# Laying out the large weights on the host so that a load's share of each partition is one run

## The reference, cut to what matters

```
mod = silu(c) @ w_ada + b_ada                      # w_ada 1024 x 6144
h = rmsnorm(x) * (1 + scale1) + shift1
q_A, k_A, v_A, f_A, q_B, k_B, v_B = split(h @ w_in) # w_in 1024 x 3080
oA = forgetting attention (prompt causal; samples over 2048 paged past rows)
oB = dilated window attention (samples over a window buffer, which is returned shifted by one row)
x = x + gate1 * (concat(rmsnorm(oA), rmsnorm(oB)) @ w_o)   # w_o 1024 x 1024
h2 = rmsnorm(x) * (1 + scale2) + shift2
s = sigmoid(h2 @ w_router); 8 of 64 experts per row, limited by groups
routed = sum over the chosen experts e: gate * (silu(h2 @ w_gate[e]) * (h2 @ w_up[e])) @ w_down[e]
shared = (silu(h2 @ ws_gate) * (h2 @ ws_up)) @ ws_down
x = x + gate2 * (routed + shared)
```

## Time and profile before

| | |
|---|---|
| time, median of 3 runs | 1496.65 us (1496.37 to 1498.79) |
| the profiled execution's own time | 1504.03 us |
| its span | 1502.3 us |
| busy share: TensorE (PE) / VectorE / ScalarE / GpSimd | 85% / 33% / 18% / 16% |
| DMA: bytes moved, mean rate | 461.85 MB, 307 GB/s |
| packets | 172315, of which 138608 on SP's queue q1 |

### The profile page before, as it was taken

How to read it: one execution, slowest core, us unless ns; L and a number is a source line. 1 busy time by engine, 2 the same in 40 slices (tenths; PEclk the granted TensorE clock), 3 DMA queues, 4 the chain that set the end, 5 groups by cost and what they waited for, 6 DMA issues and landing times.

```text
span 1502.3 us, 17576 instructions
## 1 busy us (share of the span) xinstructions
PE 1272.7 (85%) x5908; PEld 647.8 (43%) x5908; DVE 488.6 (33%) x1400; ACT 266.7 (18%) x599; POOL 244.6 (16%) x284
## 2 busy tenths in 40 slices
PE   4997899837787878788989999999899999989980
PEld 1775664314343434344434444444344444434430
DVE  2363544033443422215432222222122222222213
ACT  2221110112232234011001111111111111111110
POOL 1200000122333300000012222222122122212210
PEclk9999999968888889988999999999999999999995
DMA  9999999898989758177359999999999999999964
GB/s 356 371 336 345 354 342 341 252 371 315 390 284 383 256 199 327 42 237 255 126 193 327 334 350 363 361 356 346 360 339 336 360 339 353 351 340 357 327 198 128
DMA packets 172315, 461.85 MB, mean 307 GB/s; under 512 B 13232, under 2 KB 14512, under 8 KB 172096
## 3 DMA queue, kind: packets, MB, share of 16 engines
q1 hardware_dynamic: 138608, 349.55, 64.6%
q0 software_dynamic: 28576, 89.10, 20.5%
q10 hardware_dynamic: 5040, 22.06, 4.8%
HBM read 431.89 MB, written 106.07 MB: 358 GB/s over the span
## 4 chain that ended last, share of the span: by engine, by line
PE 65%; DMA 14%; SPq 7%; DVE 6%; issue 5%; ACT 3%; POOL 0%; POOLq 0%; DVEq 0%; ACTq 0%
PE banks L681 21%; PE banks L705 11%; PE banks L1517 6%; PE banks L537 5%; PE banks L1507 4%; DMA reg_w<-in_w_ada 4%; DMA routed_sum<-reg_w,sidx 3%; DMA reg_w<-h_rows,gidx 3%; PE banks L582 2%; SPq L1365 2%; SPq L1366 2%; PE banks L1689 1%; PE banks L690 1%; PE banks L603 1%; DMA reg_q<-in_cache_k 1%
## 5 line engine op out<-in xcount | busy, mean ns | idle before, releaser
L681 PE MATMUL banks<-reg_q,reg_w 128*128 128x512 f32 (+1 forms) x768 | 313.9, 628 | 21.1 <-issue 17.8
L681 PEld LDWEIGHTS banks<-reg_q,reg_w 128*128 128x128 f32 (+1 forms) x768 | 121.8, 177 | 188.4 <-issue 188.4
L705 PE MATMUL banks<-reg_q,reg_w 128*128 128x512 f32 (+1 forms) x384 | 154.8, 603 | 8.7 <-ACT reg_w L1199 8.7
L1298 POOL DMA_INDIRECT routed_sum<-reg_w,sidx x64 | 97.2, 1518 | 306.6 <-DMA routed_sum<-reg_w,sidx 163.7
L1055 DVE SCALAR_TENSOR_TENSOR reg_w<-banks,small,reg_w 128x256 f32<-128x256 f32 x52 | 25.1, 483 | 342.4 <-ACT reg_w L1194 342.4
L1294 POOL DMA_INDIRECT reg_w<-h_rows,gidx x52 | 55.2, 1062 | 455.6 <-DVE gidx L1015 423.7
L681 PE MATMUL banks<-hT,reg_w 128*128 128x512 f32 (+1 forms) x256 | 122.3, 634 | 6.9 <-issue 6.9
L1194 ACT ACTIVATE reg_w<-banks 128x256 f32<-128x256 f32 x52 | 19.9, 384 | 464.5 <-PE banks L681 464.5
L1517 PE MATMUL banks<-hT,reg_q 128*128 128x260 f32 x384 | 89.1, 392 | 2.4 <-DVE hT L1773 1.6
L1067 DVE COPY reg_w<-banks 128x512 f32<-128x512 f32 x52 | 35.9, 691 | 163.2 <-PE banks L705 163.2
L705 PEld LDWEIGHTS banks<-reg_q,reg_w 128*128 128x128 f32 (+1 forms) x384 | 55.6, 170 | 70.2 <-issue 58.5
(11 more groups left out here) (371 smaller groups left out, 1456.2 us busy)
## 6 DMA issues: line engine op xcount, KB each, us to landing
reg_q<-in_w_gate_up SPq DMA_DIRECT2D x48, 2048.0 KB, 20.6
reg_q<-in_w_down SPq DMA_DIRECT2D x48, 1024.0 KB, 22.9
hT<-in_w_gate_up SPq DMA_DIRECT2D x16, 2048.0 KB, 26.3
out_win_k_s<-in_win_k SPq DMA_DIRECT2D x8, 4094.0 KB, 38.6
reg_w<-in_w_ada SPq DMA_DIRECT2D x11, 2048.0 KB, 26.5
reg_w<-in_w_down SPq DMA_DIRECT2D x16, 1024.0 KB
out_win_v_s<-in_win_v SPq DMA_DIRECT2D x4, 4094.0 KB, 36.0
out_win_v_s<-in_win_v ACTq DMA_DIRECT2D x4, 4094.0 KB, 18.5
```

The source lines that it names most:

```text
L681: last = mm(pb[j % 2][of, :], lhsT=xT[:, j % 2, k, of], rhs=wgu[LOAD[p] % 4][:, k, :], start=(k == 0), stop=(k == KC - 1))
L705: last = mm(pb[6 + hh][of, :], lhsT=aT[:, j % 2, c, of], rhs=wdn[LOAD[p] % 4][:, c, hh * 512:hh * 512 + 512], start=(c == 0), stop=(c == 1))
L1298: nc.gpsimd.indirect_dma_start(rsum, bass.IndirectOffsetOnAxis(ap=idx[0:of.stop - of.start, :], axis=0), y[of, u, :], None, bounds_check=T ...
```

## The change

The host's `layout` stores every large weight in the order in which a load writes it to the partitions: for each load and each partition all its numbers one after the other. A load is then 128 runs, one per partition, of 16 KB (w_ada, w_in and w_o groups, gate and up) or 8 KB (w_down, ws_down). The bytes loaded, the loads, their order, their waits and their place in on-chip memory stay as they are; no engine's instruction moves. In SP's program the 8x512 numbers per partition of a load become 4096 in one run.

```diff
         def sync_after(sp):
             sp.wait_ge(aux_free, NAUX)
             for s in range(2):
-                sp.dma_start(wslot[s], I["w_o"][:, s * 512:s * 512 + 512].rearrange("(k p) n -> p k n", p=P)
-                             ).then_inc(group_in[s], 16)
+                sp.dma_start(wslot[s].rearrange("p a b -> p (a b)"), I["w_o"][s]).then_inc(group_in[s], 16)
...
             def load_gu(u, w):
-                sp.dma_start(wgu[u], w.rearrange("(k p) n -> p k n", p=P)).then_inc(wgu_in[u], 16)
+                sp.dma_start(wgu[u].rearrange("p a b -> p (a b)"), w).then_inc(wgu_in[u], 16)
 
             def load_dn(u, w):
-                sp.dma_start(wdn[u], w.rearrange("(c p) n -> p c n", p=P)).then_inc(wdn_in[u], 16)
+                sp.dma_start(wdn[u].rearrange("p a b -> p (a b)"), w).then_inc(wdn_in[u], 16)
...
-                load_gu(n % 4, I["w_gate_up"][ds(expert, 1), :, :].rearrange("a k n -> (a k) n"))
+                load_gu(n % 4, I["w_gate_up"][ds(expert, 1), :, :].rearrange("a p n -> (a p) n"))
...
             def load_group(which, n):
                 b = BUFFER[which, n]
-                at = 512 * n if which == "ada" else win_cols[n]
-                sp.dma_start(wslot[b], I["w_" + which][:, at:at + 512].rearrange("(k p) n -> p k n", p=P)
-                             ).then_inc(group_in[b], 16)
+                sp.dma_start(wslot[b].rearrange("p a b -> p (a b)"), I["w_" + which][n]).then_inc(group_in[b], 16)
...
+    def tiled(w, starts, n):
+
+        lead = w.shape[:-2]
+        w = w.reshape(lead + (-1, P, w.shape[-1]))
+        return c(np.stack([np.moveaxis(w[..., s:s + n], -2, -3).reshape(lead + (P, -1)) for s in starts]))
...
-        "w_ada": a["w_ada"][0], "w_in": a["w_in"][0],
+        "w_ada": tiled(a["w_ada"][0], range(0, 6 * D, 512), 512), "w_in": tiled(a["w_in"][0], win_cols, 512),
...
-        "w_gate_up": c(np.concatenate([a["w_gate"][0], a["w_up"][0]], -1)), "w_down": a["w_down"][0],
+        "w_gate_up": tiled(np.concatenate([a["w_gate"][0], a["w_up"][0]], -1), (0,), 2 * F)[0], "w_down": tiled(a["w_down"][0], (0,), D)[0],
```

More of the change, by code:

```diff
@@ L415, in program @@
         pv_ready, oT_copied, rl_set = sem("pv_ready"), sem("oT_copied"), sem("rl_set")
-        win_cols = [0, W, 3 * W + H, 4 * W + H, 2 * W, 5 * W + H]
         SQ0, X0, XT0, HT0 = TT + 1, TT, KC, 2 * KC + 2
@@ L1216, in sync_after @@
             for s in range(2):
-                sp.dma_start(wslot[s], I["w_o"][:, s * 512:s * 512 + 512].rearrange("(k p) n -> p k n", p=P)
-                             ).then_inc(group_in[s], 16)
+                sp.dma_start(wslot[s].rearrange("p a b -> p (a b)"), I["w_o"][s]).then_inc(group_in[s], 16)
             sp.dma_start(xres[:, :], I["x"][0:P, :]).then_inc(xres_in, 16)
-            sp.dma_start(wslot[2], I["ws_gate_up"].rearrange("(k p) n -> p k n", p=P)).then_inc(group_in[2], 16)
+            sp.dma_start(wslot[2].rearrange("p a b -> p (a b)"), I["ws_gate_up"]).then_inc(group_in[2], 16)
             def load_gu(u, w):
-                sp.dma_start(wgu[u], w.rearrange("(k p) n -> p k n", p=P)).then_inc(wgu_in[u], 16)
+                sp.dma_start(wgu[u].rearrange("p a b -> p (a b)"), w).then_inc(wgu_in[u], 16)
             def load_dn(u, w):
-                sp.dma_start(wdn[u], w.rearrange("(c p) n -> p c n", p=P)).then_inc(wdn_in[u], 16)
+                sp.dma_start(wdn[u].rearrange("p a b -> p (a b)"), w).then_inc(wdn_in[u], 16)
             for n in range(2):
@@ L1239, in sync_after @@
             sp.wait_ge(proj_ready, 2 * TT)
-            sp.dma_start(wsd, I["ws_down"].rearrange("(c p) n -> p c n", p=P)).then_inc(wsd_in, 16)
+            sp.dma_start(wsd.rearrange("p a b -> p (a b)"), I["ws_down"]).then_inc(wsd_in, 16)
             sp.wait_ge(x1_set, 2 * TT)
@@ L1254, in sync_after @@
                 sp.wait_ge(gu_ready, freed + 1)
-                load_gu(n % 4, I["w_gate_up"][ds(expert, 1), :, :].rearrange("a k n -> (a k) n"))
+                load_gu(n % 4, I["w_gate_up"][ds(expert, 1), :, :].rearrange("a p n -> (a p) n"))
                 sp.wait_ge(y_ready, 2 * freed + 2)
-                load_dn(n % 4, I["w_down"][ds(expert, 1), :, :].rearrange("a k n -> (a k) n"))
+                load_dn(n % 4, I["w_down"][ds(expert, 1), :, :].rearrange("a p n -> (a p) n"))
             sp.wait_ge(m_over, 1)
@@ L1264, in sync_after @@
                         sp.wait_ge(oh_set, i * NE + (NU + 1 + p))
-                        sp.dma_start(wgu[0], I["w_gate_up"][ds(expert, 1), :, :].rearrange("a (k p) n -> (a p) k n", p=P)
+                        sp.dma_start(wgu[0].rearrange("p a b -> p (a b)"), I["w_gate_up"][ds(expert, 1), :, :].rearrange("a p n -> (a p) n")
                                      ).then_inc(m_in, 16)
-                        sp.dma_start(wdn[0], I["w_down"][ds(expert, 1), :, :].rearrange("a (c p) n -> (a p) c n", p=P)
+                        sp.dma_start(wdn[0].rearrange("p a b -> p (a b)"), I["w_down"][ds(expert, 1), :, :].rearrange("a p n -> (a p) n")
                                      ).then_inc(m_in, 16)
@@ L2136, in layout @@
     cols = lambda g: g.reshape(KC, P).T
+    def tiled(w, starts, n):
+        lead = w.shape[:-2]
+        w = w.reshape(lead + (-1, P, w.shape[-1]))
+        return c(np.stack([np.moveaxis(w[..., s:s + n], -2, -3).reshape(lead + (P, -1)) for s in starts]))
+    win_cols = [0, W, 3 * W + H, 4 * W + H, 2 * W, 5 * W + H]
     both = lambda g: np.concatenate([g, g])
@@ L2155, in layout @@
         "win_k_seen": c(wk), "win_v_seen": c(wv),
-        "w_o": a["w_o"][0], "w_router": c(a["w_router"][0].reshape(KC, P, NE).transpose(1, 0, 2)),
-        "w_gate_up": c(np.concatenate([a["w_gate"][0], a["w_up"][0]], -1)), "w_down": a["w_down"][0],
-        "ws_gate_up": c(np.concatenate([a["ws_gate"][0], a["ws_up"][0]], -1)), "ws_down": a["ws_down"][0],
+        "w_o": tiled(a["w_o"][0], (0, 512), 512), "w_router": c(a["w_router"][0].reshape(KC, P, NE).transpose(1, 0, 2)),
+        "w_gate_up": tiled(np.concatenate([a["w_gate"][0], a["w_up"][0]], -1), (0,), 2 * F)[0], "w_down": tiled(a["w_down"][0], (0,), D)[0],
+        "ws_gate_up": tiled(np.concatenate([a["ws_gate"][0], a["ws_up"][0]], -1), (0,), 2 * F)[0],
+        "ws_down": tiled(a["ws_down"][0], (0,), D)[0],
     }
```

## The result

The changed kernel takes 1568.12 us (median of 4 runs, 1567.18 to 1568.62), against 1496.51 us before: 1.048 times as long, 95% interval 1.046 to 1.049. The forecast had the sign and the place, and half of the size: 1534 us, with 1556 as the upper end.

The account below looks back on a forecast made before the run. TensorE and DMA were taken as within 10% of each other, the gather without slack. Cycles +46, first stage -4, dry queues -5: 1496.65 + 37 = 1534 us, range 1474 to 1556 for 8 in 10.

Parts of the forecast that it names:

- the 1.8 us at the lower clock: Behind each pair's stall, TensorE standing still over 2 us comes back at the lower clock, 1.8 us more per cycle.
- the 5 us that x was said to have in hand: At the start, x lands 7 us later but its scaling has some 5 us in hand; 2 to 3 us come through.
- the 5 us taken off: Over the pairs, 5 us less loss where the weights' queue runs dry in part of the chain: +42 becomes +37.
- the 7 us carried over: Whole kernel: the median stays 7 us below the profiled execution after the change too.
- Relief for the loads: In a cycle of the routed experts, DMA demand falls from 56.2 to 53.0 us and waits for weights go.
- Turns by packet: At the DMA queues, engines take one packet from each waiting queue in turn, whatever its size; each row pays one weight packet.
- rival of cut runs: In the loads, 16 KB go out as 4 KB packets: -11 to 0 us, about 1490; chance 0.10, including effects that cancel.
- The chain of 16 rows: Behind a pair, two scatters and a gather put 16 rows per engine on the path: 5.8 us of stall per cycle.
- the mean price: Per gather or scatter row, the average weight packet rises from 104 to 467 ns, 0.36 us more.
- The first stage: Before the routed experts, cheaper loads against a later x: -4 us, ends -8 and +3.
- relief: Rival at the experts: the weights' queue is empty when scatters and gather run; 1476 us, at best 1451; chance 0.24.
- rival of scatters that bind everywhere: In every cycle, 32 rows at 0.36 us add 11.5 us: cycle of 64, worst case +100, 1590 us; chance 0.04.

Follow-up runs that it names:

- e2: The kernel before with only w_ada and w_in laid out in one run per partition, all else as before; 1505.30 us, ratio 1.0026.

## Why the prediction was wrong, point by point

It was wrong in size: the range ended at 1556, and the measured time is 1568. Its mechanism stands. The step that failed most is the 1.8 us at the lower clock behind a stall, which measured 3.1; next come the 5 us that x was said to have in hand at the start, of which nothing was there, and two terms without a row, the 5 us taken off and the 7 us carried over.

- **Price of a packet: right.** 618 ns was taken for 16 KB, 611 measured. (The line as written, 37 ns per KB and 14 ns, gives 606; 618 comes of 37.9 and 12.)
- **Relief for the loads: right.** The demand falls, the waits for weights go from 24.7 us to nothing. The demand's sum took a gather for 128 rows of 4 KB, as the description of the kernel does. But 520 rows with 8 experts each are 4160 rows in 52 units, 80 each; for the other places the queue sends small packets. From 1250 to 1259 us q0 sent 224 packets for only 0.54 MB, which is the 64 rows of a scatter and 68 of the gather. With 20 instead of 32 rows of gathers per engine the demand of before is 54.2 us instead of 56.2, beside 55.1 measured.
- **Turns by packet: right**, at a size that the trace of before didn't hold: 70 to 69. The Trainium skill (DMA: Bandwidth & Descriptors, Queues, rings and completion order) has each engine go round its queues packet by packet; the trace agrees, with one run or row as the packet. The rival of cut runs is out: 16 KB went out whole.
- **The chain of 16 rows: right by luck, with two errors that cancel.** 5.8 us of stall per pair were forecast, 5.9 measured. But the first scatter grew from 8.2 to 10.9 us on average over the 11 pairs, by 2.6, where the mean price gave 4 x 0.36 = 1.4. Its rows stand against packets of 16 KB alone (1.15 MB / 70), and an engine sends five packets and not four: from 1240 to 1248 us q0 sent 80, 64 rows and 16 small ones. 5 x 0.53 = 2.65 fits, but is an estimate that no run tests. The part from the second scatter on grew by some 3 us (in the chain of waits a gather took 7.8 to 8.2 us before and 10.8 to 11.9 now) where the mean price gave 4.3.
- **The loss at the lower clock: mis-sized.** The step "comes back at the lower clock, 8.78 - 7.02 = 1.8 us more" was read from `up` behind waits of 2.0 to 3.3 us. The chain of waits of before also had longer ones, followed by a slower `up`:

```profile
1062.87 4.66 issue
1067.53 9.57 PE banks L681 x32
...
1338.46 4.78 issue
1343.24 9.95 PE banks L681 x32
```

  That is 2.6 and 2.9 us more, behind stalls shorter than the 5.8 forecast. In the changed kernel the cycle holds 59.6 - 50.6 - 5.9 = 3.1 us for it, and the rows show it: 0.9 in the transposes (1.97 against 1.04) and 1.9 in `down` (5.51 against 3.63). With the stall that is 59.6 per cycle instead of 58.2, 15 us over 11.
- **"I take off 5 for pairs where the queue runs dry": had no row behind it.** All 11 pairs stall. 5 us.
- **The first stage: -4 forecast, +5.3 measured** (first `up` at 772.9 against 767.6 us). What was forecast for the wait near 130 us came true: it shrank from 6.7 to 0.3 us, where 6 was to be given back. The start was wrong. x came 9.1 us late and not 7, and "the scaling has some 5 us in hand" was a misreading: it starts 7.19 us after the first read of x in both traces (16.34 to 23.53, and 25.44 to 32.63), with ScalarE's passes over x between the two. TensorE's first transpose came 5.5 us late (34.61 against 29.15), and left waiting until then, it ran all of them at the lower clock. Before, and with the change (PEclk is 1.00 and 0.50):

```profile
29.15:35.49 6.34, 6.18 (x46) 4.46 (x49) 5.09 (x8) 0.00 (x0) 0.00 (x0) 1.00 1.05 387
```
```profile
34.61:45.08 10.47, 10.30 (x45) 7.15 (x49) 6.42 (x11) 0.00 (x0) 0.00 (x0) 0.50 1.00 426
```

  They end 9.6 us late. The last work ahead of the wait near 130 us is 11.9 us late (95.05 against 83.17), and 6.4 of that the wait gave back.
- **"The difference carries over": didn't.** The profiled execution of before was 7.5 us over its median, with cycles some 0.6 us longer than in the like executions (`e2`), the one after 0.3. 7 us.

Together: experts 61 instead of 41 us, start +5 instead of -4, the end behind the last pair's `up` -2, median 7 more than the span. That is 71.6 instead of 37.

Of the rivals, relief would have needed gathers and scatters that meet an empty queue. The order of issue in the trace of before spoke against that the earlier trace rows, and all 11 pairs stall. The rival of scatters that bind everywhere is out as well: only behind pairs did TensorE wait.

## What to carry to other kernels

In all these traces the queues of an engine take turns by packet. The longer one run of a bulk load, the longer every small transfer on another queue waits for its turn, so that a change which makes the bulk cheaper can make the kernel slower. Look for the latency chain of small indirect transfers first, count its rows per engine and price each with one packet of the bulk; choose the run length where waits for bulk and waits for small transfers balance (here 4 KB), and put a transfer that everything waits for ahead of the bulk on its own queue. A stall of TensorE costs more than its length: add what the work behind it takes at the lower clock, read at the place where the stall will be and behind stalls as long as it.

## What was not expected

- A stall of 5.9 us cost TensorE 3.1 us more at the lower clock, half of the stall again, though the engine is at full clock for most of each cycle.
- 9 ns per packet and 27 GB/s per engine explain the loads' packets: 2 KB 85 ns alone, 16 KB 611 ns. The gain per byte from 2 to 16 KB is 10%, and by this line half of it is had at 4 KB.
- SP's issue of a load fell to 0.33 us (6.16 us for one in rows 10), and was still 3 to 8.6 us for most loads in 4 KB runs and mostly 0.33 to 0.38 for 8 KB runs: it goes with the number of runs. With no wait for weights left, an earlier issue had nothing to give here.
